# Tap buffers with the tap index innermost, and the spatial norm's factor and bias on VectorE

## The reference

```
z = n @ w_in;  u, v, a, gate = split(z)             # 512 columns each
v = layer_norm(v, sgu_ln_g, sgu_ln_b)               # the "spatial norm": factor and bias of 512 columns
out_a = u * (tril(W_s) v + b_s)                     # 4 heads, chunks of 128 positions
glu = a * sigmoid(gate)
c = causal depthwise conv of glu, 31 taps, + conv_b # prompt: zeros to the left; sample: state_conv to the left
out_b = silu(layer_norm(c, conv_ln_g, conv_ln_b))
o = concat[out_a | out_b] @ w_out
h = h + rms_norm(o, g_post)
```

## Time and profile before

| | us |
|---|---|
| median of 3 runs | 1705.68 (1703.89 to 1707.11) |
| profiled execution | 1702.72 |
| its span, first to last instruction | 1701.0 |
| PE busy | 1603.9 (94%) |
| DVE busy | 1027.5 (60%) |
| ACT busy | 699.6 (41%) |
| POOL busy | 203.5 (12%) |
| mean granted PE clock | 0.974 of full speed |

### The profile page before, as it was taken

The page is one execution under the profiler, slowest core; times in us unless marked ns, Lnnn a source line. Parts: engine busy times, 40 slices in busy tenths (PEclk is TensorE's granted clock), DMA queues, the critical chain, the costliest instruction groups (busy, mean ns, idle before and its releaser), DMA issues.

```text
span 1701.0 us, 28434 instructions
## 1 busy us (share of the span) xinstructions
PE 1603.9 (94%) x11770; PEld 1550.1 (91%) x11770; DVE 1027.5 (60%) x1310; ACT 699.6 (41%) x1204; POOL 203.5 (12%) x177
## 2 busy tenths in 40 slices
PE   6999999999999979997989999799999999999997
PEld 6899999999999979996978869689999999999996
DVE  4773675476467467998345442677367547646744
ACT  5451353254145354641443333445135325414532
POOL 2020120121022000004001010002012012102200
PEclk8999999999999989999999999899999999999997
DMA  4222233233223322222334452122223323322321
GB/s 145 75 86 88 75 100 100 76 100 100 75 79 97 124 83 69 90 82 93 124 104 149 149 176 82 41 75 88 87 75 100 100 76 99 100 75 76 100 75 56
DMA packets 137903, 159.16 MB, mean 94 GB/s; under 512 B 3197, under 2 KB 130769, under 8 KB 137768
## 3 DMA queue, kind: packets, MB, share of 16 engines
q1 hardware_dynamic: 132192, 138.16, 25.6%
q0 software_dynamic: 5488, 19.10, 3.2%
q10 hardware_dynamic: 96, 0.02, 0.0%
HBM read 152.22 MB, written 5.40 MB: 93 GB/s over the span
## 4 chain that ended last, share of the span: by engine, by line
PE 82%; DVE 12%; ACT 3%; issue 1%; DMA 0%; POOL 0%; ACTq 0%; DVEq 0%; POOLq 0%
PE slot L1771 40%; PE slot L1895 36%; DVE f L1581 4%; DVE wp L1210 1%; PE slot L1815 1%; ACT wp L692 1%; DVE f L1246 1%; PE slot L1799 1%; PE slot L2119 1%; DVE f L1588 1%; DVE h L1250 1%; PE slot L2138 1%; PE slot L1829 1%; DVE f L1290 1%; DVE folded L1225 1%
## 5 line engine op out<-in xcount | busy, mean ns | idle before, releaser
L1895 PE MATMUL slot<-nb,wu 128*128 128x288 f32 x4704 | 632.7, 295 | 10.6 <-issue 5.9
L1895 PEld LDWEIGHTS slot<-nb,wu 128*128 128x128 f32 x4704 | 628.4, 188 | 12.9 <-issue 8.1
L1771 PE MATMUL slot<-mid,wp 128*128 128x288 f32 x4176 | 573.6, 298 | 26.5 <-DVE wp L1210 15.1
L1771 PEld LDWEIGHTS slot<-mid,wp 128*128 128x128 f32 x4176 | 564.7, 191 | 32.3 <-issue 24.8
L692 ACT ACTIVATE wp<-raw 128x1024 fp32r<-128x1024 f32 x120 | 127.0, 1059 | 364.3 <-PE slot L1771 340.8
L1210 DVE TENSOR_TENSOR wp<-raw,wp 128x1024 fp32r<-128x1024 f32 x120 | 146.9, 1224 | 139.5 <-ACT wp L692 139.4
L610 POOL TENSOR_TENSOR raw<-raw,q 128x512 f32<-128x512 f32 x56 | 80.2, 1431 | 872.3 <-DVE wu L1346 559.9
L1771 PE MATMUL slot<-n,wp 128*128 128x288 f32 x1152 | 165.6, 304 | 12.4 <-DVE n L1232 11.9
L1771 PEld LDWEIGHTS slot<-n,wp 128*128 128x128 f32 x1152 | 159.7, 195 | 16.8 <-issue 14.4
L1474 DVE TENSOR_TENSOR f<-slot,f 128x576 f32<-128x576 f32 x48 | 36.3, 756 | 135.3 <-PE slot L1771 135.3
L1351 DVE TENSOR_TENSOR wu<-q,wu 128x1024 fp32r<-128x1024 f32 x56 | 88.0, 1572 | 24.6 <-ACT wu L807 23.4
(11 more groups left out here) (246 smaller groups left out, 1432.3 us busy)
## 6 DMA issues: line engine op xcount, KB each, us to landing
raw<-in_ffn_w_gate_dram SPq DMA_DIRECT2D x32, 1024.0 KB, 5.4
raw<-in_ffn_w_up_dram SPq DMA_DIRECT2D x32, 1024.0 KB, 5.4
raw<-in_ffn_w_down_dram SPq DMA_DIRECT2D x32, 1024.0 KB, 4.9
raw<-in_mix_w_in_dram SPq DMA_DIRECT2D x8, 1024.0 KB, 5.3
kring<-in_cache_mem_k_dram POOLq DMA_DIRECT2D x6, 1024.0 KB, 5.7
raw<-in_xattn_w_k_dram SPq DMA_DIRECT2D x4, 1024.0 KB, 4.9
raw<-in_xattn_w_v_dram SPq DMA_DIRECT2D x4, 1024.0 KB, 5.0
raw<-in_mix_w_out_dram SPq DMA_DIRECT2D x4, 1024.0 KB, 5.0
```

The source lines that it names most:

```text
L1771: ins = pe.matmul(slot(u)[:, half, 0:HALF], wp[:, J % 2, wi, kt], X(xi, kt, half), start=kt == 0 and k == 0, stop=kt == KT - 1 and k == le ...
L1895: ins = pe.matmul(dst[:, 0:HALF], wu[:, p, wi, kt], nb[:, p, xi, kt], start=start and kt == 0 and k == 0, stop=kt == KH - 1 and k == len(P ...
```

## The change

Three edits. The tap buffers become [128, 8 sequences, 8 positions, 31 taps], so ACT and DVE write them with a step of 31 floats and the sum reads them with a step of one. The norm of `sv` becomes two fused steps on DVE, (v - mean) * factor and then (that) * reciprocal root + bias, for each of five tiles; POOL keeps only the two output DMAs. On ACT the first two `v4` copies move behind Silu and its high copies.

```diff
-                   [("taps0", [P, TAPS, NB * DEC], F32), ...
+                   [("taps0", [P, NB, DEC, TAPS], F32), ...
...
         def tap_of(ct, k):
-            return taps[ct % 2][:, k, :].rearrange("p (b k) -> p b k", b=NB)
+            return taps[ct % 2][:, :, :, k]
...
-            pool.wait_ge(ld_ln, 32)
-            for i in range(TT):
-                m = token_tile(i)[1]
-                pool.wait_ge(sv_n, i + 1)
-                nc.gpsimd.tensor_tensor(sv[0:m, i], sv[0:m, i], lng[0:m, :], ALU.mult).then_inc(sv_g, 1)
-                pool.wait_ge(sv_g, i + 1)
-                nc.gpsimd.tensor_tensor(sv[0:m, i], sv[0:m, i], lnb[0:m, :], ALU.add).then_inc(sv_b, 1)
             pool.wait_ge(sv_b, TT)
...
             root_spread("cvar")
-            for t in range(2):
-                copy_job("v4", t, vT[:, 4 + t], MEM)
             for t in range(CT):
                 act.wait_ge(cn_ready, t + 1)
                 nc.scalar.activation(f[:, 4 + t], f[:, 4 + t], ACT.Silu, scale=clg[t], bias=clb[t]).then_inc(act_b, 1)
             for t in range(CT):
                 act.wait_ge(act_b, t + 1)
                 nc.scalar.activation(mid[:, 0, 4 + t], f[:, 4 + t], ACT.Copy).then_inc(mid_hi, 1)
+            for t in range(2):
+                copy_job("v4", t, vT[:, 4 + t], MEM)
...
-                    V.tensor_reduce(f[:, 4 + ct, SEQ:T], taps[ct % 2][:, :, :].rearrange("p k n -> p n k"), AX_X, ALU.add)\
+                    V.tensor_reduce(f[:, 4 + ct, SEQ:T], taps[ct % 2][:, :, :, :].rearrange("p b k n -> p (b k) n"), AX_X, ALU.add)\
...
                 V.reciprocal(vrs[0:64, 4:5], vrs[0:64, 4:5]).then_inc(sv_rs, 1)
+                dve.wait_ge(ld_ln, 32)
+                for i in range(TT):
+                    m = token_tile(i)[1]
+                    V.scalar_tensor_tensor(out=sv[0:m, i], in0=sv[0:m, i], scalar=bag[0:m, 2 * i:2 * i + 1], in1=lng[0:m, :],
+                                           op0=ALU.subtract, op1=ALU.mult).then_inc(sv_n, 1)
                 dve.wait_ge(sv_rs, 1)
                 for i in range(TT):
                     m = token_tile(i)[1]
-                    V.tensor_scalar(sv[0:m, i], sv[0:m, i], bag[0:m, 2 * i:2 * i + 1], vrs[0:m, i:i + 1],
-                                    ALU.subtract, ALU.mult).then_inc(sv_n, 1)
+                    dve.wait_ge(sv_n, i + 1)
+                    V.scalar_tensor_tensor(out=sv[0:m, i], in0=sv[0:m, i], scalar=vrs[0:m, i:i + 1], in1=lnb[0:m, :],
+                                           op0=ALU.mult, op1=ALU.add).then_inc(sv_b, 1)
```

More of the change, by code:

```diff
@@ L222, in build @@
                    [("prob", [P, 2, HEADS, MEM], F32), ("k3", [P, MT, D], F32), ("qs", [P, KT, 2, 4 * 40], F32)],
-                   [("taps0", [P, TAPS, NB * DEC], F32), ("spare0", [P, 4 * T - TAPS * NB * DEC], F32),
+                   [("taps0", [P, NB, DEC, TAPS], F32), ("spare0", [P, 4 * T - TAPS * NB * DEC], F32),
                     ("lng", [P, SGW], F32), ("lnb", [P, SGW], F32), ("straw", [120, 2, CW], F32),
-                    ("taps1", [P, TAPS, NB * DEC], F32), ("spare1", [P, 8 * T - 2 * SGW - 2 * CW - TAPS * NB * DEC], F32)])
+                    ("taps1", [P, NB, DEC, TAPS], F32), ("spare1", [P, 8 * T - 2 * SGW - 2 * CW - TAPS * NB * DEC], F32)])
         rf = views("region_f", [("f", [P, KT, T], F32)],
@@ L315, in normed_to @@
             return sums[s][x], (int(s[-1]) - 1) * each + count
-        sv_st, sv_mv, sv_rt, sv_rs, sv_n, sv_g, sv_b = (
-            sem(x) for x in ("sv_st", "sv_mv", "sv_rt", "sv_rs", "sv_n", "sv_g", "sv_b"))
+        sv_st, sv_mv, sv_rt, sv_rs, sv_n, sv_b = (sem(x) for x in ("sv_st", "sv_mv", "sv_rt", "sv_rs", "sv_n", "sv_b"))
         conv_step, cc_ready, cn_ready, act_b = (sem(x) for x in ("conv_step", "cc_ready", "cn_ready", "act_b"))
```

## The result

The changed kernel takes 1692.62 us in the median of five runs (1690.01 to 1697.08); the kernel before, five runs on the same chip, 1705.68 (1702.11 to 1707.11). The ratio is 0.9934, with a 95% interval of 0.9918 to 0.9950: faster by 0.66%, or 11.3 us (8.5 to 14.0). The forecast was 1695.7 us, 10.0 us less. The profiled execution of the changed kernel is the slowest of its five, 1697.1 us with a span of 1695.3, so the two spans differ by 5.7 us only. That is no contradiction, for both ends lie outside the change. The spread of the norm that opens token mixing (`pre2`) starts at 646.5 us in the profile of before and at 650.4 here, 3.9 us later, and what lies behind the first output job took 877.4 us against 875.3, though its instructions are the same. In between the changed kernel is 11.7 us shorter. I therefore compare stretches counted from that spread, not positions.

The account below looks back on a forecast made before the run. DVE's late arrival, leaving PE idle 7.6 us before `cmean`'s second half, was the bound. 9.2 us there plus 0.8 from ACT's order: 1702.7 - 10.0 + 3.0 = 1695.7 us; range 1692 to 1698.5, wider 1692 to 1701.

Parts of the forecast that it names:

- The bound: Before `cmean`'s second half: PE waits 7.6 us for DVE, so DVE savings pay in full up to 7.6 us.
- The four reductions: Convolution sums (L1588) on DVE: reading with a step of one float cuts each from 3.63 to 2.24 us, 5.6 saved.
- The norm: Spatial norm: ten DVE steps take 6.63 us, 1.4 more; without POOL's work four convolution steps get 3.1 us back.
- The slack of `take_u(3)`: DVE's `take_u(3)` at 758.43: 3.1 us of slack against 2.8 us of gain, so the early gain just survives.
- The taps' writes: ACT's 120 strided tap writes (L1009): about 50 ns more each, no cost on the path; DVE's four at most 0.2 us.
- Rival 2: Strided ACT tap writes become the bound; 0.4 us more each would give 1709.0 us, slower than before; chance 0.04.
- One of the forecast's signs: ACT's tap writes: L1009 stays under 400 ns; past 500 ns the forecast would fall.
- The order on ACT: Before the first output job: PE's 0.82 us wait goes, only the weights' load is late next; 0.8 us gained.
- Rival 3: First output job: weights land 3 us later than reckoned, PE waits 1.7 us, giving 1698.2 us; chance 0.08.
- The end of `cmean`: PE's second half of `cmean` takes 2.1 us at the high clock and ends at 787.3, not 796.5: 9.2 us earlier.
- The clock behind it: Spread of the variance and `v4` jobs behind `cmean`: taken as now, the spread 2.30 us at granted clock 0.50.
- rival 4: PE's clock: later dip gone, 1694.7 us or less; low level still at `cmean`'s end, 1697.6; within the forecast's 0.77.

Follow-up runs that it names:

- eight added steps: Changed kernel with eight needless 128x512 DVE steps behind the norm; ratio 0.9984, median 1701.27 us.
- the row of steps: Kernel before, its four reductions reading the same 64 groups of 31 elements with steps of 1, 2, 4 and 16 floats; executed once, time not used.
- the added products: Changed kernel with ten unused 128x512 products on GpSimd, starting with the norm's fused steps; ratio 0.9991, median 1702.19 us.
- norm-only: Kernel before with only the spatial norm's factor and bias moved to DVE; ratio 0.9989, median 1702.22 us.
- order-only: Kernel before with only the two `v4` copies moved behind Silu on ACT; ratio 0.9996, median 1702.82 us.
- the earlier reciprocal: Changed kernel with DVE's reciprocal of the variance after the second head's gating, not the third's; two measurements, ratios 0.9915 and 0.9909.

## Why the prediction was right, step by step

- **The bound.** Right. DVE's time ahead of 792.5 went into PE's hole one for one: eight added steps, 6.2 us, gave 6.2 us of hole.
- **The four reductions.** 2.24 us expected, 2.22 measured, and it is the step, as the row of steps shows. The single rate that the Trainium skill (VectorE: DVE Perf Modes, the perf-mode tier table) has for tensor_reduce holds for dense reads only: they take the 2.22 us that the prediction had estimated with that page's formula for fp32 tensor_tensor. The note on cachelines of the Trainium skill (SBUF — State Buffer, Door 1) wants at least two hits on a 16-byte line for full bandwidth, and the jump between steps of 2 and 4 floats agrees. The note also says that fp32 can stride 4 for free; read as a step of 4 floats, that isn't so here, where such a step took 3.79 us against 2.21.
- **The norm.** 6.63 us expected, 6.6 measured, without idle time of DVE in it. The stretched steps fell from 5.75 to 2.65 as reckoned, and the added products brought the stretching back. DVE reached the end of the convolution 7.4 us earlier, counted from `pre2` (145.97 to 138.53); 7.3 had been forecast. GpSimd's two output DMAs left 16.0 us earlier, counted from `pre2`, and held nothing up: the six convolution steps beside them took 3.98 us.
- **The slack of `take_u(3)`.** Held, just: DVE had no idle time there. A term was missing: as DVE comes earlier PE no longer waits 0.5 us for the split of u3's weights (that wait is in the norm-only and the order-only profile, not in the changed one). With it PE finishes the first half of `cmean` 0.7 us earlier, so the hole is 0.9 us and not 0.3. It costs nothing, since DVE sets the end.
- **The taps' writes.** 50 ns more each expected, 63 measured (DVE's four: 42 more); no wait on the path came of it. Rival 2 needed 330. One of the forecast's signs was missed by this: L1009 was to stay under 400 ns and took 406.
- **The order on ACT.** The 0.82 us went, and the load is what ACT waits for now, as forecast (3.61 us idle until the output weights landed). Not resolved in the times. Rival 3's price was reckoned wrong: a wait of 1.7 us puts the time 1.7 us above the forecast, 1697.4, and 1698.2 counts the lost 0.8 twice. The range doesn't hang on it.
- **The end of `cmean`.** 9.2 us earlier expected, to be read from DVE's first step behind it: 796.52 - 646.50 = 150.0 against 791.21 - 650.39 = 140.8. That is 9.2, with a little luck: DVE gave 7.4 and not 7.3, the matmuls 1.8 and not 1.9.
- **The clock behind it.** This is the term that was mis-sized. The prediction took the spread and the `v4` jobs "as now", 2.30 and 14.41 us; both profiles of the changed kernel have 1.25 and 13.81. That is 1.65 us more gain, the favourable side of rival 4. 9.2 + 0.8 + 1.65 = 11.7, and the stretch is 11.7 us shorter in both; the ratio gives 11.3 (8.5 to 14.0), which can't tell 10.0 from 11.7. Nor is this gain assured: with the old order on ACT and the same hole of 0.9 us the dip was there, whole.

The parts alone sum to 0.38 + 0.11 + 0.04 = 0.53%, the whole is 0.66%. The intervals leave room for chance. But the profiles show a reason too: their stretches are 7.1, 1.1 and 0.5 us shorter, 8.8 in all against 11.7 for the whole, and 1.7 of the missing 2.9 us is the second dip, which each part alone kept and the whole had in neither of its profiles. What decides whether that dip comes stays open. In all profiles of the table but the two with the earlier reciprocal PE stands some 2 us before the spread, for the reciprocal; those two had no dip, nor had the two of the changed kernel, and all others had it.

## What to carry over

Look for the place where the engine that bounds the kernel stands idle, and cost every edit by what arrives there; an engine at 60% busy was the bound for 100 us. Order a float32 buffer so that the engine on the path reads it dense (steps of 4 and 8 bytes cost the same here, 16 bytes cost 1.7 times as much), and let an engine with slack write it strided. Work on GpSimd isn't free beside a busy VectorE: with two SBUF inputs each, they take turns, and giving VectorE 1.4 us more of its own work saved it 3.1 us of turns.

## What the runs showed of the hardware beyond that

- A VectorE reduction of 1984 float32 takes 2.21 us with a step of 4 or 8 bytes, and 3.5 to 3.8 us with 16, 64 or 256. A ScalarE write of 64 float32 takes 63 ns more with a step of 124 bytes than dense, 1.0 ns an element.
- GpSimd can be shut out for as long as VectorE runs two-input steps back to back (11.57 us for one product), and only then slows it.
- A hole of 7.0 us on PE in place of 0.9 came with 3.7 us of clock on top: 2.0 in the matmuls right behind it and 1.7 in a second dip some 10 us later. The second is not tied to a long hole: it stood whole behind one of 2.9 us and, in one profile of five, behind one of 0.9.
- That second dip has one size and no fixed place: 1.7 us in eight profiles, while the spread, the first of the two pieces it can fall on, took anything from 1.25 to 2.29 us. Parts with the same instructions also differ from one execution to the next: what lies behind the first output job took 871.6 to 877.6 us in the twelve profiles, and `pre2`'s spread came between 645.1 and 650.9 us. An effect under 5 us is to be read within a stretch, or from medians, never from two spans.
